# First RMS norm: from a stage of its own into the attention's input projection

## The reference, cut to what matters

```python
mod_x = silu(c) @ w_ada[l] + b_ada[l]          # also for c_ctx: six vectors of 1024
z_x = modulate(rms_norm(x, g_norm1[l]), sh1, sc1) @ w_in[l]
z_c = modulate(rms_norm(xc, g_norm1[l]), csh1, csc1) @ w_in[l]
# rms_norm(t, g) = t * rsqrt(mean(t*t) + eps) * g ;  modulate(h, sh, sc) = h * (1 + sc) + sh
```

## Time and profile before

| | us |
|---|---|
| median of 3 runs (lowest, highest) | 4143.54 (4136.83, 4148.22) |
| the profiled execution's own time | 4128.93 |
| its span in the profile | 4127.1 |
| layer 0: norm stage, then projection stage | 0 to 61, 61 to 182 |
| layer 1: norm stage, then projection stage | 2242 to 2280, 2280 to 2377 |

### The profile page before, as it was taken

The page is one execution under the profiler, slowest core; times in us unless marked ns, Lnnn a source line. Parts: engine busy times, 40 slices in busy tenths (PEclk is TensorE's granted clock), DMA queues, the critical chain, the costliest instruction groups (busy, mean ns, idle before and its releaser), DMA issues. The chain is left out here.

```text
span 4127.1 us, 65802 instructions
## 1 busy us (share of the span) xinstructions
PE 3651.8 (88%) x27258; PEld 2030.6 (49%) x27258; DVE 2224.7 (54%) x3676; ACT 1062.2 (26%) x2344; POOL 491.2 (12%) x675
## 2 busy tenths in 40 slices
PE   6899999677897699999997899998697875999998
PEld 4555575566733233333333655674486532333333
DVE  2454224687755644444443445334778757565654
ACT  3342010544311111111112443112534221212121
POOL 1100000221201011111111200000232110110100
PEclk8999999688998799999998899999698987999999
DMA  6300120200175677777774000121100326999996
GB/s 229 125 1 11 56 77 0 79 13 19 44 278 206 228 261 261 262 261 262 262 255 120 33 21 11 59 69 36 54 10 13 114 103 250 329 333 330 333 329 204
DMA packets 291447, 613.12 MB, mean 149 GB/s; under 512 B 37544, under 2 KB 45992, under 8 KB 284496
## 3 DMA queue, kind: packets, MB, share of 16 engines
q1 hardware_dynamic: 270608, 542.32, 36.9%
q0 software_dynamic: 20544, 66.60, 6.3%
HBM read 561.07 MB, written 47.79 MB: 148 GB/s over the span
## 5 line engine op out<-in xcount | busy, mean ns | idle before, releaser
L3014 PE MATMUL ps<-moe_w,e_hT 128*128 128x512 f32 x1024 | 451.1, 598 | 17.4 <-issue 9.2
L3143 DVE TENSOR_TENSOR moe_w<-moe_w 128x2048 f32<-128x2048 f32 x128 | 287.1, 2285 | 204.0 <-PE ps L2945 159.2
L2915 PE MATMUL ps<-moe_w,e_xs 128*64 128x512 f32 x1536 | 348.6, 596 | 0.8 <-DVE moe_w L3143 0.8
L2915 PE MATMUL ps<-moe_w,e_xT 128*64 128x512 f32 x1536 | 343.7, 597 | 0.7 <-DVE moe_w L3143 0.7
L3014 PEld LDWEIGHTS ps<-moe_w,e_hT 128*128 128x128 f32 x1024 | 192.9, 191 | 255.5 <-issue 252.7
L3149 DVE TENSOR_TENSOR e_cb<-e_part,ps 128x512 f32<-128x512 f32 x128 | 87.7, 685 | 335.2 <-ACT e_part L3051 249.3
L2915 PEld LDWEIGHTS ps<-moe_w,e_xT 128*64 128x64 f32 x1536 | 111.4, 138 | 221.3 <-issue 221.2
L2915 PEld LDWEIGHTS ps<-moe_w,e_xs 128*64 128x64 f32 x1536 | 105.4, 137 | 193.7 <-issue 192.3
L1207 PE MATMUL ps<-M 96*128 96x512 f32 (+1 forms) x400 | 182.6, 543 | 3.5 <-PEq L913 2.1
L3051 ACT COPY e_part<-ps 128x512 f32<-128x512 f32 x96 | 56.3, 586 | 479.8 <-PE ps L2915 471.5
L1097 PE MATMUL ps<-yT,hT 128*128 128x272 f32 (+1 forms) x608 | 146.6, 396 | 9.6 <-PEq L262 9.2
(11 more groups left out here) (424 smaller groups left out, 7093.8 us busy)
## 6 DMA issues: line engine op xcount, KB each, us to landing
moe_w<-in_w_gate_dram SPq DMA_DIRECT2D x128, 1024.0 KB, 13.9
moe_w<-in_w_up_dram SPq DMA_DIRECT2D x128, 1024.0 KB, 14.1
moe_w<-in_w_down_dram SPq DMA_DIRECT2D x128, 1024.0 KB, 13.0
o_mod_w<-in_w_ada_dram SPq DMA_DIRECT2D x24, 1024.0 KB, 7.9
m_mod_w<-in_w_ada_dram SPq DMA_DIRECT2D x16, 1024.0 KB, 5.8
yT<-in_w_in_dram SPq DMA_DIRECT2D x6, 2048.0 KB, 7.9
r_z<-z_rows SPq DMA_DIRECT2D x20, 512.0 KB, 3.4
z_rows<-p_zo POOLq DMA_DIRECT2D x36, 256.0 KB, 2.3
```

Source lines behind the costliest of these rows:

```text
L2915: ins = nc.tensor.matmul(ps[HF * q:HF * q + HF, b, :], x[:, k], weights[q][:, k], start=(first and k == 0), stop=(k == 3), skip_group_chec ...
L3014: ins = nc.tensor.matmul(ps[:, YB + c, :], hT2[:, 4 * half + k], quarter(name, e)[:, k], start=(half == 0 and k == 0), stop=(half == 1 and ...
L3143: nc.vector.tensor_tensor(to, a, b, ALU.subtract).then_inc(*td.up())
```

## The change

`stage_norm1` and its call are gone. Its steps are written into `stage_project_mla`, so that tile j+1 is turned in iteration j and tile j+3 is squared and scaled there:

- Row buffers `xb` (three) and `xn` (two) lie in the first half of `g.yT`; sums, means, coefficients get buffers of their own.
- The turns of a tile's two halves use one bank, 5. Both products of `keys_values` use bank 1, so each waits for the scaling of the tile before.
- PE: `x_turned(j+1, 0)`, then `project(j, 1)`, latent turned, heads, `x_turned(j+1, 1)`, then `project(j, 0)` and the rest. `x_turned(t, 0)` waits for the scaled rows and for DVE's eviction of tile t-1, `x_turned(t, 1)` for ACT's eviction of half 0.
- ACT evicts half 0 at the head of an iteration and squares tile j+3 at its end. DVE evicts half 1 after the latent scaling and scales tile j+3 after the heads' scaling. Both evictions apply scale and shift, in both layers.
- Layer 0: the first modulation block is now block 0 of `ModRows` (eight loads of 1 MB, ring of three, one bias broadcast of 12 parts for all three blocks), worked before tile 0 is turned; the silu, the bias sum, the turn and the coefficients come before the loop.
- SP: in layer 0 the columns of c, c_ctx and the gain, three weight loads, row tile 0, the biases, five weight loads, row tile 1; in layer 1 row tile 0, the coefficient columns, row tile 1. Then the projection's weights in two column halves (second half first), row tile 2, the small tables, and the other row tiles with the later modulation loads between them.

```diff
-MOD_PREP = [(0, 2 * D), (0, 4 * D)]
+MOD_PREP = [(0, 0), (0, 2 * D), (0, 4 * D)]
...
-        ZBANK, KV = (6, 7), (1, 5)
+        ZBANK, KV, XB = (6, 7), (1, 1), 5
...
@@ sync
+                def x_load(t):
+                    if t >= 3:
+                        sp.wait_ge(*xnd.at(t - 2))
+                    sp.dma_start(xb[:, t % 3], g.x_rows(I, l, t)).then_inc(*x_in[t % 3].up(16))
+                if first:
+                    with nc.allow_non_contiguous_dma(reason="vectors into columns"):
+                        sp.dma_start(cc[:, :, 0], col(I["c"][0], KT)).then_inc(*c_in.up(16))
+                        sp.dma_start(cc[:, :, 1], col(I["c_ctx"], KT)).then_inc(*c_in.up(16))
+                        sp.dma_start(gn[:], col(I["g_norm1"][l], KT)).then_inc(*c_in.up(16))
+                    for j in range(3):
+                        mod.load(sp, j)
+                    x_load(0)
+                    mod.load_bias(sp)
+                    for j in range(3, MOD_LOADS):
+                        mod.load(sp, j)
+                    x_load(1)
+                else:
+                    x_load(0)
...
+                    x_load(1)
+                for a, cols in ((1, slice(HALF, W_MLA)), (0, slice(0, HALF))):
+                    sp.dma_start(w[:, :, cols], wsrc[:, :, cols]).then_inc(*w_in[a].up(16))
+                x_load(2)
...
+                for t in range(3, NT):
+                    x_load(t)
+                    if mod and t == 3:
+                        for j in range(MOD_LOADS, MOD_LOADS + 3):
+                            mod.load(sp, j)
+                    if mod and t >= 6:
+                        for j in range(MOD_LOADS + 2 * t - 9, MOD_LOADS + 2 * t - 7):
+                            mod.load(sp, j)
@@ scalar
+                x_squares(0)
+                x_squares(1)
+                x_out(0)
+                x_squares(2)
                 for j in range(NT + 3):
+                    if j + 1 < NT:
+                        x_out(j + 1)
...
                         keys_values(j - 1)
+                    if j + 3 < NT:
+                        x_squares(j + 3)
@@ vector
                     if j < NT:
                         latent(j)
+                    if j + 1 < NT:
+                        x_out(j + 1)
                     if 1 <= j <= NT:
                         head_variance(j - 1)
                         normed(j - 1)
+                    if j + 3 < NT:
+                        x_scaled(j + 3)
@@ tensor
-                    if t >= 2:
-                        pe.wait_ge(*scaled.at(t - 1))
-                        pe.wait_ge(*hsq.at(t - 1))
+                    if t >= 1:
+                        pe.wait_ge(*scaled.at(t))
+                        pe.wait_ge(*hsq.at(t))
...
+                x_turned(0, 0)
+                x_turned(0, 1)
                 for j in range(NT + 3):
+                    if j + 1 < NT:
+                        x_turned(j + 1, 0)
                     if j < NT:
                         project(j, 1)
                     if 1 <= j <= NT:
                         latent_turned(j - 1)
                     if j >= 3:
                         heads(j - 3)
+                    if j + 1 < NT:
+                        x_turned(j + 1, 1)
                     if j < NT and has_q(j):
                         project(j, 0)
```

More of the change, by code:

```diff
@@ L889, in stage_project_mla @@
         ones = sg("coef")
-        mod = ModRows(nc, g, I, sb, MOD_PREP, 4, 3) if l == 0 else None
-        ZBANK, KV = (6, 7), (1, 5)
+        first = l == 0
+        spare = g.yT[:, 0:4].rearrange("p a n -> p (a n)")
+        xb = spare[:, 0:3 * D].rearrange("p (a n) -> p a n", a=3)
+        xn = spare[:, 3 * D:5 * D].rearrange("p (a n) -> p a n", a=2)
+        xjunk = sb("xjunk", [P, D])
+        xss = sb("xss", [P, NT])
+        xrs = sb("xrs", [P, NT])
+        mc = sb("mc", [P, 2, 2, KT])
+        gn = sb("gn", [P, KT])
+        G = sb("G", [P, 2, KT])
+        x_in, w_in, c_in = [sg(f"w_slot{i}") for i in range(3)], [sg("nx_weights0"), sg("nx_weights1")], sg("nx_columns")
+        xsq, xvr, xrq, xnd, xtr = sg("nx_squares"), sg("nx_mean"), sg("nx_root"), sg("nx_scaled"), sg("nx_turned")
+        xea, xed, xcd = sg("nx_evac_a"), sg("nx_evac_d"), sg("nx_coef")
+        mod = ModRows(nc, g, I, sb, MOD_PREP, 4, 3) if first else None
+        silu_done, mtr = sg("silu_done"), sg("mod_tr")
+        cc = sb("cc", [P, KT, 2]) if first else None
+        ZBANK, KV, XB = (6, 7), (1, 1), 5
+        n_coef = 3 if first else 2
         def has_q(t):
@@ L1124, in heads, with x_turned @@
                         ins.then_inc(*tr[i].up())
+                def x_turned(t, half):
+                    if half == 0:
+                        pe.wait_ge(*xnd.at(t + 1))
+                        if t:
+                            pe.wait_ge(*xed.at(t))
+                    else:
+                        pe.wait_ge(*xea.at(t + 1))
+                    for k in range(4):
+                        ins = nc.tensor.transpose(ps[:, XB, k * P:(k + 1) * P], xn[:, t % 2, (4 * half + k) * P:(4 * half + k + 1) * P], g.ident)
+                    ins.then_inc(*xtr.up())
+                if first:
+                    pe.wait_ge(*silu_done.at(1))
+                    for j in range(MOD_LOADS):
+                        mod.product(pe, j)
+                    pe.wait_ge(*mod.used.at(1))
+                    for i in range(4):
+                        ins = nc.tensor.transpose(ps[:, XB, i * P:(i + 1) * P], mod.rows[:, 0, i * P:(i + 1) * P], g.ident)
+                    ins.then_inc(*mtr.up())
+                    pe.wait_ge(*xcd.at(n_coef))
+                x_turned(0, 0)
+                x_turned(0, 1)
                 for j in range(NT + 3):
+                    if j + 1 < NT:
+                        x_turned(j + 1, 0)
                     if j < NT:
@@ L1137, in _ @@
                     if mod and 2 <= j < NT:
-                        mod.product(pe, 2 * j - 4)
-                        mod.product(pe, 2 * j - 3)
+                        mod.product(pe, MOD_LOADS + 2 * j - 4)
+                        mod.product(pe, MOD_LOADS + 2 * j - 3)
         sg.settle()
```

244 lines of the change are left out of this document (72 added, 172 removed).

## The result

The changed kernel takes 4105.27 us (median of 10 runs, 4095.47 to 4127.43) and the kernel before, in the same set, 4135.71 us (10 runs, 4118.41 to 4148.22): ratio 0.9937, 95% interval 0.992 to 0.9954. So it is faster, by 0.46% to 0.8%. The sign and the mechanism of the forecast held.

The account below looks back on a forecast made before the run. It took layer 0's norm stage as DMA-bound except its tail, layer 1's as an engine chain, the loops as PE-bound. Layer 0's -9.5 and layer 1's -9.0 made -18.5 us, scaled to 4125.0 us; range 4114 to 4142.

Parts of the forecast that it names:

- layer 0, start: Layer 0 up to the first projection: it starts at about 44.1 instead of 61.08, a gain of 17.0 us.
- layer 0, loop: Layer 0's projection loop: eight more transposes per tile at 0.88 us, nine iterations, the first half-price, 7.5 us more.
- layer 1, start (to tile 2's projection): Layer 1 up to tile 2's projection: it starts at about 2273.4 instead of 2289.32, a gain of 15.9 us.
- layer 1, loop and end: Layer 1 from tile 2 on: transposes and late DVE eviction cost 6.7 us, the wait at the end 0.2 us.
- one bank at the end: End of layer 1's loop: `keys_values` waits about 2.4 us for its single bank, mostly behind DVE's rotation, costing 0.2 us.
- the projection of tile 1 (at the lower clock level 3.96): Layer 1's start: tile 1's projection was taken to last 3.96 us, ahead of tile 2's projection.
- Rival 1: Both layers: starts gain only 13 + 11 us, loops cost 15; gain 9 us, 4134.5 us, chance 0.26.
- Rival 2: Both loops: turns wait for evictions on one bank, 3.3 us per tile; 41 us slower, 4185 us, chance 0.09.
- Rival 3: Layer 0's start: small loads are slow, eight take 4.6 us longer; gain 13.9 us, 4129.6 us, chance 0.05.
- Rival 4: Both layers: starts reach their upper bounds and DVE costs nothing; gain 26 us, 4117.5 us, chance 0.11.
- I apply the ratio: 4143.54 x (1 - 0.0045): Whole kernel: the 0.45% saving on the profiled execution is applied to the shown runs' median, giving 4125.0 us.
- 4 us for the spread of the runs: Whole kernel: allowance of 4 us for run spread, added to rival 4 to set the range's lower end, 4114.

Follow-up runs that it names:

- experiment 3: Changed kernel with both halves of tile j+1 turned at the head of iteration j, still on one bank: 4167.23 us, ratio 1.0079 to the kernel before.
- experiment 4: Changed kernel with rows squared and scaled two tiles ahead instead of three: 4228.92 us, ratio 1.0217 to the kernel before.

## Why the prediction was right or wrong

Terms of the sum against the profiles (a negative term is time saved, and the terms are rounded; means over the four profiles with the new stage and the three with the old one in each layer):

| term | forecast | first pair | means |
|---|---|---|---|
| layer 0, start | -17.0 | -16.6 | -17.3 |
| layer 0, loop | +7.5 | +6.6 | +6.5 |
| layer 1, start (to tile 2's projection) | -15.9 | -17.5 | -19.0 |
| layer 1, loop and end | +6.9 | +7.7 | +7.6 |
| sum | -18.5 | -19.9 | -22.1 |

- **Layer 0's start was right**, step by step: products at 11.7, 14.1, 16.6, 23.5 and 33.7 (forecast 11.2, 13.7, 16.2, 23 and 33), the bias parts at 3.2 us (I had taken 3), the chain behind them 9.1 forecast and 8.9 measured (35.6 to 44.5). That the chain fits so closely is in part luck: in the other three profiles with this stage it takes 7.6, 8.0 and 8.9 us, depending on the clock level in it.
- **The loops' mechanism was right**: eight transposes cost 0.83 us per tile (0.88 forecast), with no wait in layer 0. In layer 1 DVE's eviction is late where the sum had it, though on two tiles only, by 0.7 and 0.3 us, instead of 0.2 on each of five; the sum is the same 1.0, and from tile 2's projection to the last one the cost is 6.7 us as forecast (73.81 against 67.14). The **one bank at the end** was mis-sized: "0.2 us" measured 1.0. The wait of 4.25 us lies not quite beside the rotation: DVE then stands idle for 0.90 us until the squares of the late product are there, and before it had no idle time at this place. The layer 0 loop came out 0.9 us cheaper; half of that is the smaller cost per tile, and the other half I did not trace.
- **Layer 1's start was undersized by 3 us.** Two things: "the projection of tile 1 (at the lower clock level 3.96)" took 2.34 us, and this brings tile 2's projection from 31.3 to 29.7 us behind the stage's start. That level was not certain either: 4.01 us in the kernel with the biases late. And the base came from one execution in which the old stages stood at 47.2 us; two others have 48.2 and 49.3. One profile has an error of its own of about 1 us per stage. Against the gain, the first projection stood 15.0 us behind the start and not 14.0, since the coefficient columns take SP 0.9 us each (3.64 for four) and not "0.6", and row tile 1 is issued behind them.
- **Rival 1** asked for lower bounds of the starts and for loops of 15 us; the starts came in at 34 to 36 us. Its reading of the clock was off too: a granted clock of 0.60 between two levels of 1.0 and 0.5 means four fifths of that time at the lower one, not "half of TensorE's work". **Rival 2** did not occur, but experiment 3 shows that the mechanism is real: a single bank turned without cover makes the kernel slower than before. Its price, 59 us, is near the 64.6 of the stages, but not by its own working of 3.3 us per tile everywhere: a tile became 1.8 us longer in layer 0 and some 5 in layer 1, part of it the clock. What decides is the place of the second turn in PE's list. **Rival 3** did not occur: 2.36 to 2.73 us per load of 1 MB. The page "DMA: Bandwidth & Descriptors" of the Trainium skill, section "Bandwidth", has 341 GB/s for a transfer of 1 MB, measured with transfers issued from GpSimd; here it is 1.05 MB in 2.5 us, 420 GB/s, issued by SyncE with three loads in flight. The measurement decides for this kernel. **Rival 4** (26 us) is nearest to what was timed: 4135.71 x (1 - 0.9937) is 26 us. Its reason is not what happened, though, since only layer 1's start came in at its upper bound.
- **What failed is the last step, "I apply the ratio: 4143.54 x (1 - 0.0045)" and the range from it.** The miss is 19.7 us (4125.0 against 4105.27). Of these 7.8 us are the base: the three runs shown had a median of 4143.54, where ten have 4135.71, and later sets 4138.98, 4138.45 and 4138.42. 3.6 us are the terms above. The remaining 8.3 us are in the medians themselves: they differ by 30.4 us, where the means of the same ten and ten runs, whose ratio is the 0.9937, differ by 26.0 and the stages give 22.1. What these 8.3 us are stays open; the interval of the ratio allows that they are scatter. With 4135.71 as the base the same sum gives 4117.2 and a range from 4106, which the time would have missed by 1 us. The changed kernel's own medians in three sets of runs are 4105.27, 4112.06 and 4106.29; all three are below the range's 4114. "4 us for the spread of the runs" was too little, when the three runs shown already spanned 11 us and the profiled execution stood 14.6 us below their median: that said that the base was high. A range around a ratio needs the uncertainty of the base in it, which here is about as large as the uncertainty of the sum.

## What to carry to other kernels

A stage that only prepares can be woven into a PE-bound loop if each of its steps on PE finds its operand ready one projection earlier: with the turns split around the other work and rows scaled three tiles ahead it saves 22 us, with the turns together it loses 33 us, with two tiles ahead it loses 90 us. Cut both traces at the borders of unchanged code and compare the pieces: the changed stages repeated within 1 to 3 us, while ten runs of one kernel spanned about 30 us. When the forecast is a ratio of a few tenths of a per cent, give the base of three runs a width of its own.

## What the runs showed of the hardware that I had not expected

- A wait can cost more than its length. Behind a wait of 4.80 us the projection took 6.18 instead of 3.83 us (experiment 4), behind one of 3.06 us 5.07 (experiment 3, layer 1), behind 1.60 us 3.83 in the loop of layer 0. The length of the one wait does not settle it: in the sparser layer 1 start of experiment 3 a projection behind 1.60 us took 5.52, and behind the same 2.46 us tile 1's projection took 2.34 us in four profiles and 4.01 in a fifth. The first projection of layer 0 took 4.79 to 5.99 us in four profiles of the same stage, and 5.89, 6.13 and 6.46 in the three kernels in which it starts earlier; the two ranges touch, so that an earlier start is given back in part is likely, not shown.
- Small broadcasts are dear for their bytes: twelve of 64 KB delayed a queue of 1 MB loads by 3.2 us, where 0.79 MB at the loads' pitch would be 1.9. Four of them in between two loads delayed these by 1.6 us (products 3.31 and 3.25 us apart instead of 2.50).
- Unchanged code scatters more than the effect of half the change. Over all thirteen profiles, with the same code between the two stages, that stretch took 2050.87 to 2070.69 us, and the last one 1746.93 to 1762.02. Single stages behind the changed one moved too: the attention of layer 0 192.4 to 197.9 us, the retention of layer 1 69.8 to 77.0.
